# A hybrid encoder layer: the last two stages joined to the feed-forward

## What is computed

```
hf = rmsnorm(x, norm_ffn_g)
x = x + (silu(hf @ w_gate) * (hf @ w_up)) @ w_down      # D_FF = 2816
g = sigmoid(rmsnorm(x, norm_ple_g) @ w_ple_gate)         # 1024 x 1024
x = x + g * (p @ w_ple)                                  # p: 1152 x 256
y = rmsnorm(x, final_norm_g)
```

## Time and profile before

| | us |
|---|---|
| median of 3 runs (2755.94 to 2760.21) | 2759.9 |
| the profiled execution | 2755.53 |
| its span | 2753.8 |
| PE busy | 2637.9 (96%) |
| DVE busy | 1526.8 (55%) |
| ACT busy | 852.4 (31%) |
| POOL busy | 348.2 (13%) |

### The profile page before, as it was taken

One profiled execution on the slowest core, in us unless ns is written; L12 is line 12 of the kernel. 1 busy time (PEld: TensorE's weight loads), 2 busy tenths in 40 slices (PEclk: granted clock), 3 DMA queues, 4 the chain that ended last, 5 costly groups with the idle time before them and its releaser, 6 DMA issues. The chain is left out here.

```text
span 2753.8 us, 48010 instructions
## 1 busy us (share of the span) xinstructions
PE 2637.9 (96%) x17088; PEld 2509.4 (91%) x17088; DVE 1526.8 (55%) x2581; ACT 852.4 (31%) x1566; POOL 348.2 (13%) x327
## 2 busy tenths in 40 slices
PE   6999999999979999999979999999999999999798
PEld 6888888888869989999979999999999999999697
DVE  5665765676654757675753443444544444444645
ACT  4443434343332524343441122211111111111443
POOL 0222322232221111111100002000000000000400
PEclk9999999999989989999989999999999999999799
DMA  5444444376523142436346433311111111111012
GB/s 139 90 104 76 117 83 108 73 105 88 113 46 48 25 98 33 99 32 95 37 163 205 170 99 124 124 46 39 43 41 40 43 40 44 38 46 38 30 40 93
DMA packets 331854, 214.31 MB, mean 78 GB/s; under 512 B 117828, under 2 KB 312216, under 8 KB 331672
## 3 DMA queue, kind: packets, MB, share of 16 engines
q1 hardware_dynamic: 331672, 211.98, 33.4%
HBM read 164.51 MB, written 47.41 MB: 77 GB/s over the span
## 5 line engine op out<-in xcount | busy, mean ns | idle before, releaser
L162 PE MATMUL bank<-operand_hi,w_hi 128*128 128x384 f32 x1584 | 532.6, 336 | 1.8 <-DVE w_lo L144 1.5
L162 PE MATMUL bank<-operand_hi,w_lo 128*128 128x384 f32 x1584 | 529.8, 334 | 0.0
L162 PE MATMUL bank<-operand_lo,w_hi 128*128 128x384 f32 x1584 | 529.8, 334 | 0.0
L137 ACT ACTIVATE w_hi<-w_raw 128x1024 fp32r<-128x1024 f32 x171 | 180.6, 1057 | 794.5 <-PE bank L162 490.3
L162 PEld LDWEIGHTS bank<-operand_hi,w_hi 128*128 128x128 f32 x1584 | 297.5, 188 | 2.6 <-issue 2.4
L162 PEld LDWEIGHTS bank<-operand_lo,w_hi 128*128 128x128 f32 x1584 | 297.5, 188 | 0.3
L162 PEld LDWEIGHTS bank<-operand_hi,w_lo 128*128 128x128 f32 x1584 | 297.4, 188 | 0.0
L144 DVE TENSOR_TENSOR w_lo<-w_raw,w_hi 128x1024 fp32r<-128x1024 f32 x171 | 211.9, 1240 | 139.8 <-ACT w_hi L137 138.7
L682 PE MATMUL acc<-operand_hi,w_hi 128*128 128x384 f32 x792 | 281.5, 355 | 5.5 <-PEq L212 5.5
L1054 POOL TENSOR_TENSOR wgt<-wgt,left 128x128 f32<-128x128 f32 (+2 forms) x224 | 210.7, 947 | 575.4 <-DVE left L1011 405.6
L162 PE MATMUL sacc<-operand_hi,w_hi 128*128 128x384 f32 x768 | 268.7, 350 | 4.9 <-DVE w_lo L144 3.8
(11 more groups left out here) (319 smaller groups left out, 4492.3 us busy)
## 6 DMA issues: line engine op xcount, KB each, us to landing
w_raw<-in_w_in SPq DMA_DIRECT2D x65, 512.0 KB, 8.7
k_cache<-in_cache_k SPq DMA_DIRECT2D x256, 64.0 KB, 2.5
v_cache<-in_cache_v SPq DMA_DIRECT2D x64, 256.0 KB, 4.7
w_raw<-in_w_gate SPq DMA_DIRECT2D x22, 512.0 KB, 3.8
w_raw<-in_w_up SPq DMA_DIRECT2D x22, 512.0 KB, 3.9
w_raw<-in_w_down SPq DMA_DIRECT2D x22, 512.0 KB, 3.7
s_gate_a<-gate SPq DMA_DIRECT2D x24, 192.0 KB, 2.9
s_o<-o_t SPq DMA_DIRECT2D x8, 576.0 KB, 10.1
```

The costliest lines, as they stand in the source:

```text
L137: act.activation(S.w_hi[u0 % 2][:, :], S.raw[u0 % 2][:, :], ACT.Copy).then_inc(S.hi_done, 1)
L162: last = pe.matmul(acc[:, 0:RBN], w[:, k, :], a[:, k, rows], start=(n == 0), stop=(n == 3 * kts - 1 and more is None))
```

## The change

`stage_ple` and `stage_final` become one `stage_end` in the same program block as the feed-forward, without a border of all engines between them.

- p is loaded ahead of x at the start of the feed-forward, turned by PE behind "up0" and between the first blocks of "up1" of its first pass, and split by ACT and DVE there.
- The first gate tile and the first embedding tile get split buffers of their own (`first_gate_w`, `first_emb`; the former lies where `f_hid` was). They are split within the last down pass, after blocks 2 and 5 on ACT, 4 and 7 on DVE; embedding tiles are split over their 256 columns alone.
- From block 12 of the last down pass on, the down blocks use banks 0 to 2. After each group of three, PE runs two k steps of the first gate tile for all three row blocks in banks 3 to 5 (`first_gate`), each as soon as the low part of its k is there; two of the three first embedding blocks stand before the last step.
- The column sums, root and reciprocal come behind that; each row block's reciprocal is followed by its scaling. Passes 1 to 5 remain a loop; gate banks are 3 to 5, embedding banks 0 to 2.
- Output tiles 6 and 7 are done by row block: gate 6, embedding 6, gate 7, embedding 7, in banks 0 and 1 in turn. Their weights have four buffers. The three row tiles of a block that is finished are turned back together, behind the first gate block of the next, and squared, scaled and stored there, in PSUM tiles of banks 2 to 7.
- For the last three row tiles seven of eight k are turned and squared first, the last k after that.
- `sq_sums` is allocated earlier and `stream` is freed before the feed-forward, for room.

```diff
@@ -129,20 +129,23 @@
-    def split_hi(self, act, u0, per, i, last_block):
+    def split_hi(self, act, u0, per, i, last_block, cols=D, home=None):
 
         S = self.S
+        hi = S.w_hi[u0 % 2][:, 0:cols] if home is None else home[0]
         act.wait_ge(S.raw_in[u0 % 2], (u0 // 2 + 1) * 16 + i * (per // 2 * 16))
-        act.wait_ge(S.acc_done, last_block)
-        act.activation(S.w_hi[u0 % 2][:, :], S.raw[u0 % 2][:, :], ACT.Copy).then_inc(S.hi_done, 1)
-
-    def split_lo(self, dve, u0, per, i, last_block):
+        if last_block is not None:
+            act.wait_ge(S.acc_done, last_block)
+        act.activation(hi, S.raw[u0 % 2][:, 0:cols], ACT.Copy).then_inc(S.hi_done, 1)
+
+    def split_lo(self, dve, u0, per, i, last_block, cols=D, home=None):
 
         S = self.S
+        hi, lo = (S.w_hi[u0 % 2][:, 0:cols], S.w_lo[u0 % 2][:, 0:cols]) if home is None else home
         dve.wait_ge(S.hi_done, HEAD + u0 + 1 + i * per)
-        dve.wait_ge(S.acc_done, last_block)
-        dve.tensor_tensor(S.w_lo[u0 % 2][:, :], S.raw[u0 % 2][:, :], S.w_hi[u0 % 2][:, :].bitcast(F32),
-                          ALU.subtract).then_inc(S.lo_done, 1)
+        if last_block is not None:
+            dve.wait_ge(S.acc_done, last_block)
+        dve.tensor_tensor(lo, S.raw[u0 % 2][:, 0:cols], hi.bitcast(F32), ALU.subtract).then_inc(S.lo_done, 1)
 
...
@@ -2119,27 +2122,36 @@
+    p_hi, p_lo, rstd = S.p_hi, S.p_lo, sb("rstd", [P, ROWS])
     gs = [sb(f"gs{n}", [P, RBN]) for n in range(3)]
     sg = [sb(f"sg{n}", [P, RBN]) for n in range(3)]
+    with ExitStack() as start:
+        p_rows = start.enter_context(nc.sbuf_tensor("p_rows", [P, RT, PLE], F32))
+    sb, bank, sem = tools(nc, S, own, "f")
+    first_emb = [sb(f"first_emb_{n}", [P, 2 * P], F32R)[:, :] for n in ("hi", "lo")]
+    act_hi, act_lo = sb("act_hi", [P, 2, ROWS], F32R), sb("act_lo", [P, 2, ROWS], F32R)
+    with ExitStack() as up_down:
+        hid = [up_down.enter_context(nc.sbuf_tensor(f"f_hid{n}", [P, ROWS], F32)) for n in range(2)]
+    first_gate_w = [sb(f"first_gate_{n}", [P, D], F32R)[:, :] for n in ("hi", "lo")]
     squares = gs + sg
     acc, sums = S.bank[0:6], S.bank[6:8]
...
         sp.wait_ge(S.acc_done, HEAD + b0)
+        sp.dma_start(p_rows[:, 0:PT, :], A.p_prompt[0, 0].rearrange("(r p) c -> p r c", p=P)).then_inc(p_in, 16)
...
-                pe.wait_ge(S.acc_read_v, HEAD + bv0 + b - 5)
+                pe.wait_ge(S.acc_read_v, HEAD + bv0 + b - (2 if final and n >= 15 else 5))
...
+                a = acc[n % 3 if final and n >= 12 else slot("down", n)]
...
+                if final and n >= 12 and rb == 2:
+                    first_gate(pe, 2 * (d - 4), acc[3:6], HEAD + bv0 + blk(N, "down", 9) - 6)
+                    if d == KT - 1:
+                        first_emb_block(pe, 0)
+                        first_emb_block(pe, 1)
+                    first_gate(pe, 2 * (d - 4) + 1, acc[3:6], HEAD + bv0 + blk(N, "down", 9) - 6)
+
+        def turn_p(m):
+            pe.wait_ge(p_in, 32)
+            if m >= 2:
+                pe.wait_ge(plo_done, m - 1)
+            else:
+                pe.wait_ge(var_done, 3)
+            for r in range(3):
+                last = pe.transpose(sums[m % 2][:, r * P:(r + 1) * P],
+                                    p_rows[:, 3 * (m // 2) + r, (m % 2) * P:(m % 2 + 1) * P], S.ident[:, :])
+            last.then_inc(pt_done, 1)
 
...
+        turn_p(0)
+        turn_p(1)
         for n in range(6):
             up(0, "up1", n)
+            if n < 2:
+                turn_p(2 * n + 2)
+                turn_p(2 * n + 3)
...
         split(u0 + 3, 2, 0, HEAD + b0 + 6)
+        for m in range(6):
+            act.wait_ge(pt_done, m + 1)
+            act.activation(p_hi[:, m % 2, rb_cols(m // 2)], sums[m % 2][:, 0:RBN], ACT.Copy).then_inc(phi_done, 1)
         highs(0, 0)
...
-            if d % 4 == 3:
-                split(u + d // 4, 2, 0, b + 3 * d + 3)
+            if d == 0:
+                S.W.split_hi(act, u, 2, 0, b + 3, home=first_gate_w)
+            if d == 1:
+                S.W.split_hi(act, u + 1, 2, 0, None, cols=2 * P, home=first_emb)
+            if d == 3:
+                split(u + 2, 2, 0, b + 12)
+            if d == 7:
+                S.W.split_hi(act, u + 3, 2, 0, b + 24, cols=2 * P)
...
+                if n % 12 == 11 and not final:
+                    S.W.split_lo(dve, u0 + 8 + n // 12, 6, i - 1, b + n + 1)
+                if final:
+                    u = u0 + 4 + 6 * (N - 1) + 2
+                    if n == 4:
+                        S.W.split_lo(dve, u, 2, 0, None, home=first_gate_w)
+                    if n == 7:
+                        S.W.split_lo(dve, u + 1, 2, 0, None, cols=2 * P, home=first_emb)
+                    if n == 14:
+                        S.W.split_lo(dve, u + 2, 2, 0, b + 12)
+                    if n == 23:
+                        for m in range(24 - LAG, 24):
+                            low_last(m)
...
+        for st in S.x_stored:
+            dve.wait_ge(st, DMA_HEAD + 16 * KT // 2)
+        for m in range(6):
+            dve.wait_ge(phi_done, m + 1)
+            dve.tensor_tensor(p_lo[:, m % 2, rb_cols(m // 2)], sums[m % 2][:, 0:RBN],
+                              p_hi[:, m % 2, rb_cols(m // 2)].bitcast(F32), ALU.subtract).then_inc(plo_done, 1)
...
-def stage_ple(nc, S, A, b0, bv0, u0):
...
-def stage_final(nc, S, A):
...
+def stage_end(nc, S, A, ctx, b0, bv0, u0):
...
+    gates, embs, sums = S.bank[3:6], S.bank[0:3], S.bank[6:8]
+    yt = S.pair[1:4]
...
+    def last_weights(e):
+
+        return ((*slot_parts(u0 % 2), u0 + 12), (*slot_parts((u0 + 1) % 2), u0 + 13),
+                (*last_gate, u0 + 14), (*last_emb, u0 + 15))[e]
+
+    def product(pe, a, hi, lo, rhs, rb, kts, k0=0, k1=None):
+        k1 = kts if k1 is None else k1
+        wh, wl = [w[:, 0:kts * P].rearrange("p (k c) -> p k c", k=kts) for w in (hi, lo)]
+        for k in range(k0, k1):
+            for m, (w, r) in enumerate(((wh, rhs[0]), (wh, rhs[1]), (wl, rhs[0]))):
+                last = pe.matmul(a[:, 0:RBN], w[:, k, :], r[:, k, rb_cols(rb)],
+                                 start=(k == 0 and m == 0), stop=(k == kts - 1 and m == 2))
+        if k1 == kts:
+            last.then_inc(S.acc_done, 1)
+
+    def first_gate(pe, k, banks, free):
+
+        for rb in range(NRB):
+            if k == 0:
+                pe.wait_ge(S.lo_done, HEAD + u0 + 1)
+                pe.wait_ge(S.acc_read_v, free + rb + 1)
+            pe.wait_ge(xg_done, 3 * k + rb + 1)
+            product(pe, banks[rb], *f.first_gate, (S.R0_hi, S.R0_lo), rb, KT, k, k + 1)
+
+    def first_emb_block(pe, rb):
+        if rb == 0:
+            pe.wait_ge(plo_done, 6)
+            pe.wait_ge(S.lo_done, HEAD + u0 + 2)
+        pe.wait_ge(S.acc_read_v, HEAD + bv0 - 2 + rb)
+        product(pe, embs[rb], *f.first_emb, (p_hi, p_lo), rb, 2)
+
+    def sync(sp):
+        sp.wait_ge(S.acc_done, HEAD + b0)
+        sp.dma_start(gain, A.final_norm_g.unsqueeze(0).to_broadcast([P, D])).then_inc(gain_in, 16)
+        with sp.Fori(0, N - 2) as i:
+            for j in range(2):
+                S.W.load(sp, u0 + 4 + j, 2, i, ple_tile(A, i + 2, j))
...
+    def tensor(pe):
+        for rb in range(NRB):
+            pe.wait_ge(ss_done, 3 * KT - 2 + rb)
+            if rb == 2:
+                pe.wait_ge(var_done, 1)
+            pe.matmul(sums[rb % 2][:, 0:RBN], S.ones[:, :], S.ss[:, rb_cols(rb)], start=True, stop=True)\
+              .then_inc(sum_done, 1)
+
+        def emb_block(i, rb, free):
+            pe.wait_ge(S.lo_done, HEAD + u0 + 2 * i + 2)
+            pe.wait_ge(S.acc_read_v, HEAD + bv0 + free)
+            product(pe, embs[rb], *slot_parts((u0 + 1) % 2), (p_hi, p_lo), rb, 2)
+
+        first_emb_block(pe, 2)
+        with pe.Fori(1, ND2) as i:
+            for rb in range(NRB):
+                pe.wait_ge(S.lo_done, HEAD + u0 + 2 * i + 1)
+                pe.wait_ge(S.acc_read_v, HEAD + bv0 + 6 * (i - 1) + rb + 1)
+                product(pe, gates[rb], *slot_parts(u0 % 2), (S.R0_hi, S.R0_lo), rb, KT)
+            for rb in range(NRB):
+                emb_block(i, rb, 6 * (i - 1) + 3 + rb + 1)
+
+        def turn(r, k0=0, k1=KT):
+            if k0 == 0:
+                if r >= 3:
+                    pe.wait_ge(out_done, r - 2)
+                else:
+                    pe.wait_ge(S.acc_read_v, HEAD + bv0 + 6 * ND2)
+            for k in range(k0, k1):
+                if k == 0:
+                    pe.wait_ge(mul_done, START + 3 * ND2)
+                if k >= ND2:
+                    pe.wait_ge(mul_done, START + 3 * ND2 + 2 * (r // 3) + k - ND2 + 1)
+                last = pe.transpose(yt[r % 3][:, k * P:(k + 1) * P], x[:, k, r * P:(r + 1) * P], S.ident[:, :])
+            last.then_inc(t_done, 1)
+
+        for rb in range(NRB):
+            for e in range(4):
+                hi, lo, u = last_weights(e)
+                pe.wait_ge(S.lo_done, HEAD + u + 1)
```

(80 more changed lines are left out.)

## The result

The changed kernel takes 2731.4 us (median of 4 runs, 2729.0 to 2734.9) against 2760.1 for the kernel before on the same chip (4 runs, 2756.0 to 2761.6): ratio 0.9896, interval 0.9879 to 0.9914. Two further comparisons gave 0.9911 (0.9892 to 0.9929) and 0.9896 (0.9879 to 0.9912). The forecast was 2739 with a range from 2732 to 2747: right in sign, 7.6 us short in size, the time 0.6 us under the range. Slow executions (one of the changed kernel at 2938 us with a clock of 0.84, one of before at 7185 us, both in the second comparison) are left out of the medians and ratios.
The profiled execution took 2731.04 us, its span 2729.3: 24.5 us less than the profiled one of before, where the sum said 21.0.

The account below looks back on a forecast made before the run. The prediction took PE as the bound wherever it has work, the handover and part of the tail being winnable. Its terms, mainly -25.5 handover and -7.4 tail, summed to -21.0 us, giving a 2739 us median, range 2732 to 2747.

Parts of the forecast that it names:

- the sum: Whole kernel: handover, sums, waits, restart, loop exit, transposes, down stalls, tail and p add up to -21.0 us of span.
- Bounds and the handover: Last down pass to end: PE bounds wherever it has work; the 25.5 us handover goes, a 2.7 us scaling wait comes.
- The walk: Joined last down pass, block by block: 42.9 us, with 39.5 for 228 matmuls, 2.1 slow start and 1.3 stalls.
- rival (b): Joined down pass: VectorE with GpSimd becomes the bound, +3 to +6 us, 2742 to 2745; chance 0.1.
- Leaving the loop: Loop exit: PE waits 2.9 us for the fifth pass's embedding reads before the first row block.
- rival (a): Gaps of 2.7 and 2.9 us: the clock falls at one or both, 2.2 us each, 2741 to 2743.5; chance 0.22.
- Row blocks and tail: After the loop: row blocks without stalls, 5.5 us of transposes added; last output 12.6 us after last matmul, tail -7.4.
- (c): Row blocks don't overlap as meant: PE held up to 3 us per group, tail near 23, 2744 to 2748; chance 0.06.
- (d): Row blocks and tail: a table switch costs twice its 1.28 us, +5 with the tail, 2744; chance 0.02.
- p at the front: Feed-forward start: p's 18 transposes, 2.1 us, partly fill an idle 0.27, net +1.8 us; bounds 0.5 to +4.
- Its own signs: Wrong if gate steps wait over 2 us, PE idles at p, 0.32 us matmuls follow gaps, or span change outside 15-26.
- Rival (f): Gaps of 2.7 and 2.9 us are better hidden, neither in full, and p costs 0.5: 2734; chance 0.08.

Follow-up runs that it names:

- the two repeats: The changed kernel run twice more with nothing changed: 2733.4 us (ratio 0.9911 to the kernel before) and 2731.1 us (ratio 0.9896).
- pool_small: Changed kernel with GpSimd's adds of squares cut from 384 to 48 columns; joined pass start to second pass 48.4 us instead of 50.05.
- p_later: Changed kernel with p's tiles 2 to 5 turned behind blocks 1 and 3 of the first row block instead of 0 and 1; 2730.0 us, ratio 0.9901.
- code_shift: Kernel before with five empty TensorE instructions ahead of the feed-forward, tiles unmoved; loop down pass 25.26 us, 60 unrolled distances 10.60 us against 10.40.
- best: Changed kernel with p turned later, the row blocks' first bank freed, and column sums ahead of the last gate step; 2726.5 us, ratio 0.9877.
- null_before: The kernel before under another name, nothing changed; 2761.8 us, ratio 0.9998.

## Why the prediction was right and wrong

**What put the time under the range.** The failed step is the sum's silence on the stages that the diff doesn't touch: it has no term for the ten turns of the feed-forward loop and none for the stages ahead, and gives no reason why they should stay. The runs showed -4.5 us in the loop, from another place of its tiles, and -3.7 ahead of it (5.5 in the means of all profiles; most of it a wait for keys near 693 us, its cause open). The second failed step ends the sum: "The profiled execution lies 4.4 under the median of 2759.9, so the median becomes 2738.9": it took the offset of one execution for a property of the kernel, but spans of the kernel before were 2753.8 and 2761.7, and between the change of the span and that of the medians lie 4.2 us. Together these are 12.4 us too little. The joined pass with its wait, exit and tail, and p were forecast 1.2, 1.1 and 2.5 too cheap; these 4.8 hid part of the miss, and 7.6 are left. That the miss is no larger is luck.

**Bounds and the handover.** Right. The 25.5 us went. From the last down pass to the second pass 50.05 us were measured and 48.9 forecast, the wait for the first scaled read was 2.65 against 2.7, ended by the scaling as said, and the row after it was at full clock.

**The joined pass.** 43.9 against 42.9; the slow start took 1.5 where 2.1 were forecast (2.6 and 2.4 in the two repeats, whose passes took 45.1 and 45.0), so the rest is off by more. The walk kept the low parts of the earlier trace rows at 0.90 and let them fall to 0.60 towards the end; they had a mean of 1.01, alternating 0.92 and 1.36 where VectorE didn't stop. Two stalls, 0.93 and 0.56, before the gate matmuls that need the banks of down blocks 10 and 11, stand where the walk had 0.4 for block 11; its 0.2 within gate step 6 came out as 0.2. This is rival (b) in small, 1 us and not 3 to 6. pool_small shows its cause.

**Inside the passes.** 78.47 us for the loop, 78.4 forecast; 80.0 in the four profiles where the clock fell before the second pass.

**Leaving the loop.** The wait was there and ended by an embedding read, 2.17 us against 2.9. But the clock fell behind it, which is half of rival (a): 1.5 us, not the 2.2 taken from the longer restart of the earlier trace rows. Together 3.7 against 2.9.

**Row blocks and tail.** No stall between row blocks, so (c) fell; table loads cost 1.28 and the next operation came 0.02 behind, so (d) fell. The last output ended 13.0 us behind the last matmul of a product, 12.6 forecast. From the loop's end to the end of the span 56.6 against 55.5; the clock and the exit account for 0.8 of it.

**p at the front.** Here a step of the mechanism failed, though it didn't put the time under the range: "They take up an idle 0.27 us that PE has there waiting for the first scaled read; net +1.8". It counted PE's transposes and ScalarE's copies and left out that the third group waits for VectorE's first low part, behind seven microseconds of other work. +4.3, and 5.9 in the two repeats, where the clock fell too; p_later gave 2.9 of the 4.3 back. The bound, +4, was too low as well.

**Its own signs.** Two of those named for being wrong appeared: PE idle in the stage of p, and a gap followed by matmuls of 0.32 us, at the exit. The other two didn't: the gate steps' waits stayed under 2 us and the span changed by 24.5.

**Rival (f)** named nearly the right time, 2734, for the wrong reasons: neither gap was hidden better, and p didn't cost 0.5.

## What to carry over

Allocation is part of a diff: when buffers are added, list which tiles of untouched stages get another place, and expect a change of pace there. A group of instructions moved into a full stretch has to be walked on every engine that it waits for, the bank's reader among them, and not only on the engine that issues it. Take the size of an effect between two marks of the same pair of profiles, and the time of the whole from medians alone.

## What the runs showed of the hardware

- The place of the moving operand modulo 256 bytes went with the pace of matmuls in a loop: 25.26 us for 144 of them at 32 beyond, 24.80 at 96, 24.79 at 160, switched by padding in both kernels. In the unrolled pass either pace, 0.173 and 0.177 us a matmul, was seen with the same tiles at the same places (before and code_shift).
- A VectorE operation with its operands in SBUF took 1013 ns beside GpSimd's adds of 384 columns and 617 with these cut to 48; one with an operand in PSUM took 542 and 547.
- The length of a gap didn't decide whether PE's clock fell from 2.4 to 1.2 GHz behind it. In the ten profiles of the changed kernel and its variants it fell behind the gap of 2.17 us at the loop's exit in seven of eight, behind that of 2.65 before the second pass in four of nine, behind that of 2.58 in front of p in three of seven; such a fall costs nine or ten matmuls of 0.32 us, 1.5 us more than at full clock; behind the gap of 3.15 in best it was 16. The earlier trace rows had shown no fall after 2.78; behind null_before's gap at the same place, 2.93 us, the matmuls are 0.32 us apart:

```profile
1332.60 0.88 PE L1325 MATMUL stp<-ident,conv_out 128*128 128x128 f32 x3 [2.93 <-issue]
...
1334.87 0.52 PE L162 MATMUL sacc<-operand_lo,w_hi 128*128 128x384 f32 x1
1335.19 0.52 PE L162 MATMUL sacc<-operand_hi,w_lo 128*128 128x384 f32 x1
```
